# Hybrid decoder trunk on one core: RG gates by 64 rows, next convolutions between a pair's recurrences, joined masks and forget gate operand, an earlier weight split, another order at the end

## What is computed

```python
proj = h @ w_in         # RG x | RG gate | stick-breaking qkv | forgetting qkv | 8 forget logits | 3 merge gates
xa = causal_depthwise_conv4(rg_x) + b
r = sigmoid(block_diag(xa, w_a, b_a)); i = sigmoid(block_diag(xa, w_x, b_x))   # 16 blocks of 64 x 64
log_a = -8 * r * softplus(-lam); a = exp(log_a)
u = sqrt(-expm1(2 * log_a)) * (i * xa)
h_t = a_t * h_(t-1) + u_t                           # scan over the positions
ya = gelu(rg_gate) * h
yb = stick_breaking_attention(q, k, v)              # 8 heads of 64, strictly causal, no softmax
yc = forgetting_attention(q, k, v, log_sigmoid(fox_f + bf))   # softmax, plus the summed log forget gates
mixed = g0 * (ya @ w_rg) + g1 * (yb @ w_sb) + g2 * (yc @ w_fox)
```

## Time and profile before

| what | value |
|---|---|
| runs before | 2701.96 us median of 3 (2695.99 to 2702.55) |
| the profiled execution | 2708.77 us, its span 2707.0 us |
| mean granted TensorE clock | 0.997 |
| TensorE busy | 2655.9 us |
| VectorE, ScalarE, GpSimd busy | 1238.8, 1061.0, 1174.7 us |
| loads | 323.80 MB, mean 120 GB/s |

### The profile page before, as it was taken

How to read it: one execution, slowest core, us unless ns; L and a number is a source line. 1 busy time by engine, 2 the same in 40 slices (tenths; PEclk the granted TensorE clock), 3 DMA queues, 4 the chain that set the end, 5 groups by cost and what they waited for, 6 DMA issues and landing times.

```text
span 2707.0 us, 31703 instructions
## 1 busy us (share of the span) xinstructions
PE 2655.9 (98%) x13074; PEld 2236.0 (83%) x13074; DVE 1238.8 (46%) x1586; ACT 1061.0 (39%) x1596; POOL 1174.7 (43%) x476
## 2 busy tenths in 40 slices
PE   7999999999999999999999999999999999999998
PEld 5888897888888888888888888878888888888887
DVE  6555337866443244411155552578645422453111
ACT  6232245654443253222252222566543442522223
POOL 5555434523223435545345554444223234355442
PEclk9999999999999999999999999999999999999999
DMA  8555532222122224423245555222212122253332
GB/s 307 195 192 188 179 116 86 86 70 66 64 67 71 94 88 168 158 94 101 94 164 192 198 194 171 94 78 87 70 63 71 63 78 94 90 192 129 99 99 78
DMA packets 90832, 323.80 MB, mean 120 GB/s; under 512 B 10048, under 2 KB 12480, under 8 KB 90432
## 3 DMA queue, kind: packets, MB, share of 16 engines
q1 hardware_dynamic: 90688, 321.78, 35.2%
HBM read 319.64 MB, written 2.10 MB: 119 GB/s over the span
## 4 chain that ended last, share of the span: by engine, by line
PE 89%; DVE 6%; ACT 3%; DMA 1%; issue 1%; SPq 0%; POOL 0%; ACTq 0%; DVEq 0%
PE bank L1381 27%; PE bank L1383 27%; PE bank L1382 27%; PE bank L1419 2%; DVE e_lo L1203 2%; PE bank L1568 1%; DVE e_hi L1201 1%; PE bank L1424 1%; DVE e_f L1196 1%; DMA ada<-ada_w 1%; PE bank L1615 1%; PE bank L1580 1%; ACT h_hi L595 0%; ACT w_hi L540 0%; PE bank L1601 0%
## 5 line engine op out<-in xcount | busy, mean ns | idle before, releaser
L484 POOL TENSOR_TENSOR w_lo<-raw,w_hi 128x1024 fp32r<-128x1024 f32 x434 | 1129.6, 2614 | 1401.4 <-ACT w_hi L540 1401.0
L1381 PE MATMUL bank<-h_hi,w_hi 128*128 128x512 f32 x2224 | 868.7, 391 | 1.1 <-DVE tmp L1022 0.9
L1383 PE MATMUL bank<-h_hi,w_lo 128*128 128x512 f32 x2224 | 866.0, 389 | 0.0
L1382 PE MATMUL bank<-h_lo,w_hi 128*128 128x512 f32 x2224 | 866.0, 389 | 0.0
L540 ACT ACTIVATE w_hi<-raw 128x1024 fp32r<-128x1024 f32 x434 | 458.1, 1057 | 941.2 <-PE bank L1383 870.3
L1381 PEld LDWEIGHTS bank<-h_hi,w_hi 128*128 128x128 f32 x2224 | 418.1, 188 | 87.8 <-DVE tmp L1022 1.3
L1383 PEld LDWEIGHTS bank<-h_hi,w_lo 128*128 128x128 f32 x2224 | 417.8, 188 | 87.4
L1382 PEld LDWEIGHTS bank<-h_lo,w_hi 128*128 128x128 f32 x2224 | 418.1, 188 | 86.0
L944 DVE CUSTOM_DVE_ANT_0 ada<-ada,c_act 128x1024 f32<-128x1024 f32 x144 | 235.7, 1644 | 279.1 <-DMA ada<-ada_w 279.1
L1381 PE MATMUL bank<-g_hi,w_hi 128*128 128x512 f32 (+1 forms) x792 | 290.1, 366 | 0.0
L1383 PE MATMUL bank<-g_hi,w_lo 128*128 128x512 f32 (+1 forms) x792 | 289.4, 365 | 0.0
(11 more groups left out here) (243 smaller groups left out, 3119.6 us busy)
## 6 DMA issues: line engine op xcount, KB each, us to landing
raw<-w_units SPq DMA_DIRECT2D x440, 512.0 KB, 3.4
ada<-ada_w SPq DMA_DIRECT2D x144, 512.0 KB, 4.5
ada<-ada_w SPq DMA_DIRECT2D x8, 1024.0 KB, 17.1
x<-x_in SPq DMA_DIRECT2D x4, 512.0 KB, 6.4
wab_raw<-wab SPq DMA_DIRECT2D x2, 1024.0 KB, 5.6
y<-fin SPq DMA_DIRECT2D x8, 256.0 KB, 2.2
c_act<-c_rows SPq DMA_DIRECT2D x1, 512.0 KB, 3.7
vec<-vecs SPq DMA_DIRECT2D x3, 92.5 KB, 3.2
```

The source lines that it names most:

```text
L484: nc.gpsimd.tensor_tensor(w_lo[s][:, :, :], raw[u % RAW][:, :, :], w_hi[s][:, :, :].bitcast(F32), ALU.subtract).then_inc(unit_lo.sem, 1)
L1381: nc.tensor.matmul(o, wh, xh, start=start, stop=False, skip_group_check=True)
L1382: nc.tensor.matmul(o, wh, xl, start=False, stop=False, skip_group_check=True)
L1383: return nc.tensor.matmul(o, wl, xh, start=False, stop=stop, skip_group_check=True)
```

## The change

1. `gates`: the block-diagonal matrices become one [128, 128] operand per tile. Rows 0 to 63 hold block 0 of w_a and then of w_x, rows 64 to 127 block 1 of w_x and then of w_a. Six matmuls of 64 rows, alternating between the two row halves, write to two banks: r and i of block 0 in one, i and r of block 1 in the other. `gates_done` counts twice per tile. ScalarE takes r and i by four sigmoids of 64 partitions; the bias of i is rolled by 64 partitions on the host. The wab load, its `wab_hi` copy and `wab_lo` subtract are half as large.
2. VectorE's `rg_2`: recurrence of the pair's first tile, then the next pair's two convolutions (for the last pair `q_rest` and `k_rest`), then recurrence of the second tile. `forget_2` follows `rg_2(l, 0)`.
3. Forget gate: `wf_hi` and `wf_lo` become two column ranges (0 to 7 and 32 to 39) of one operand `wf` of 40 columns, zeroed once at the start. 16 matmuls instead of 24; VectorE adds the two row ranges of bank 7.
4. `scores`: the two diagonal blocks that lie in one bank get their mask by one matmul of 256 columns. For stick-breaking pairs three mask matmuls per head instead of four; for forgetting pairs the same, behind four with decay.
5. ScalarE: the tick of `U_WRG(2p)` moves from `q_round(l, p + 1)` to before `sb_1(l, p, 0)`.
6. End: `last_half`, `square` and `square_add` of the second half stand behind all eight tiles of the first half.

The diff, cut to its core:

```diff
@@ scalar: rg_2 @@
-                    act.wait_ge(gates_done.sem, gates_done.at(l, c + 1))
+                    act.wait_ge(gates_done.sem, gates_done.at(l, 2 * c + 2))
...
-                    A(gr[s][:, :], bank[b][:, :], ACT.Sigmoid, bias=vec[:, V_BA + c:V_BA + c + 1])\
-                        .then_inc(r_ready.sem, 1)
-                    A(gi[s][:, :], bank[b + 1][:, :], ACT.Sigmoid, bias=vec[:, V_BX + c:V_BX + c + 1])\
-                        .then_inc(i_ready.sem, 1)
+                    first, second = slice(0, HD), slice(HD, P)
+
+                    for src, bnk in ((first, b), (second, b + 1)):
+                        i = A(gr[s][src, :], bank[bnk][src, :], ACT.Sigmoid, bias=vec[src, V_BA + c:V_BA + c + 1])
+                    i.then_inc(r_ready.sem, 1)
+
+                    for dst, src, bnk in ((first, second, b), (second, first, b + 1)):
+                        i = A(gi[s][dst, :], bank[bnk][src, :], ACT.Sigmoid, bias=vec[src, V_BX + c:V_BX + c + 1])
+                    i.then_inc(i_ready.sem, 1)
@@ scalar: q_round, and the loop over the stick-breaking pairs @@
-                if 1 <= p <= 4:
-                    tick(l, u - 1)
...
                 for p in range(4):
+                    tick(l, U_WRG(2 * p))
                     sb_1(l, p, 0)
@@ scalar: end @@
-                    if h == 0 and k == 3:
-                        square(DEPTH - 1, 2, KD - 1, 1)
+                if h == 0:
+                    square(DEPTH - 1, 2, KD - 1, 1)
@@ vector: rg_2 @@
-                for c in both:
+
+                def recur(c):
...
-                    if c == KD - 2:
-                        q_rest(l, 0)
-                        k_rest(l, 0)
+
+                recur(c0)
+                if c0 + 2 < KD:
+                    rg_1(l, c0 + 2)
+                    rg_1(l, c0 + 3)
+                else:
+                    q_rest(l, 0)
+                    k_rest(l, 0)
+                recur(c0 + 1)
@@ vector: forget_1 @@
-                V.tensor_scalar(fx_a[:, :], bank[7][0:HEADS, :], b, None, ALU.add).then_inc(fx_step.sem, 1)
+                V.tensor_copy(fx_c[:, :], bank[7][QUAD:QUAD + HEADS, :]).then_inc(fx_low.sem, 1)
+                dve.wait_ge(fx_low.sem, fx_low.at(l, 1))
+                V.scalar_tensor_tensor(out=fx_a[:, :], in0=bank[7][0:HEADS, :], scalar=b, in1=fx_c[:, :], op0=ALU.add,
+                                       op1=ALU.add).then_inc(fx_step.sem, 1)
@@ vector: start, layer loop @@
+            V.memset(wf[:, :, :].bitcast(F32), 0.0).then_inc(wf_zero.sem, 1)
...
+                rg_1(l, 0)
+                rg_1(l, 1)
+                forget_1(l)
                 for c in range(0, KD, 2):
-                    rg_1(l, c)
-                    rg_1(l, c + 1)
+                    rg_2(l, c)
                     if c == 0:
-                        forget_1(l)
-                    if c == 2:
                         forget_2(l)
-                    rg_2(l, c)
@@ vector: end @@
-                    if h == 0 and k == 3:
-                        last_half(DEPTH - 1, 1)
-                    if h == 0 and k == 5:
-                        square_add(DEPTH - 1, 2, KD - 1, 1)
+                if h == 0:
+                    last_half(DEPTH - 1, 1)
+                    square_add(DEPTH - 1, 2, KD - 1, 1)
@@ tensor: gates @@
-                for j in range(2):
-                    i = mm3(bank[4 + 2 * (c % 2) + j][:, :], wab_hi[c % 2][:, j, :], wab_lo[c % 2][:, j, :],
-                            xa_hi[c % 2][:, :], xa_lo[c % 2][:, :], True, True)
-                i.then_inc(gates_done.sem, 1)
+                weights, x_a = (wab_hi[c % 2], wab_lo[c % 2]), (xa_hi[c % 2], xa_lo[c % 2])
+                for lp, rp in ((0, 0), (0, 1), (1, 0)):
+                    for j, r in enumerate((slice(0, HD), slice(HD, P))):
+                        i = nc.tensor.matmul(bank[4 + 2 * (c % 2) + j][:, :], weights[lp][r, :], x_a[rp][r, :],
+                                             start=lp == rp, stop=lp == 1, skip_group_check=True)
+                        if lp == 1:
+                            i.then_inc(gates_done.sem, 1)
@@ tensor: scores, for each head e @@
-                    for i in order:
...
+                    z = [bank[b] for b in ZB[e]]
+                    if p < 4:
+
+                        add(z[1].rearrange("p (i t) -> p i t", i=TT)[:, 0:4:3, :], ident_r[:, :],
+                            mask_sb[:, :].unsqueeze(1).to_broadcast([P, 2, P]))\
+                            .then_inc(z_done.sem, 1)
+                        for b in (2, 0):
+                            add(z[b][:, 0:P], ident_r[:, :], mask_sb[:, :]).then_inc(z_done.sem, 1)
+                    else:
+                        h = pick[:, 2 * p + e - HEADS:2 * p + e - HEADS + 1].to_broadcast([P, P])
+                        add(z[0], h, decay[:, :])
+                        add(z[0][:, 3 * P:], ident_r[:, :], mask_fx[:, :]).then_inc(z_done.sem, 1)
+                        add(z[1][:, 0:3 * P], h, decay[:, 0:3 * P])
+                        add(z[1][:, 3 * P:], h, decay[:, 0:P])
+                        add(z[1][:, 2 * P:], ident_r[:, :], mask_fx[:, :].unsqueeze(1).to_broadcast([P, 2, P])).then_inc(z_done.sem, 1)
+                        add(z[2][:, 0:2 * P], h, decay[:, 0:2 * P])
+                        add(z[2][:, P:2 * P], ident_r[:, :], mask_fx[:, :]).then_inc(z_done.sem, 1)
@@ tensor: forget gate @@
-                    i = mm3(bank[7][0:HEADS, :], wf_hi[:, k, :], wf_lo[:, k, :], h_hi[:, k, :], h_lo[:, k, :], k == 0,
-                            k == KD - 1)
+                    nc.tensor.matmul(bank[7][0:QUAD + HEADS, :], wf[:, k, :], h_hi[:, k, :], start=k == 0, stop=False,
+                                     skip_group_check=True)
+                    i = nc.tensor.matmul(bank[7][0:HEADS, :], wf_hi[:, k, :], h_lo[:, k, :], start=False,
+                                         stop=k == KD - 1, skip_group_check=True)
```

More of the change, by code:

```diff
@@ L150, in at, with trunk @@
         return count
-def trunk(nc, w_units, ada_w, vecs, wf, wab, c_rows, x_in, out):
+def trunk(nc, w_units, ada_w, vecs, wf_in, wab, c_rows, x_in, out):
     with ExitStack() as ctx:
@@ L230, in trunk @@
         gt = [at(f"gt{i}", 45056 + 2048 * i, [P, T]) for i in range(2)]
-        wab_raw = at("wab_raw", 65536, [P, KD, 2, P])
-        wab_hi = [at(f"wab_hi{i}", 73728 + 1024 * i, [P, 2, P], F32R) for i in range(2)]
-        wab_lo = [at(f"wab_lo{i}", 75776 + 1024 * i, [P, 2, P], F32R) for i in range(2)]
+        wab_raw = at("wab_raw", 65536, [P, KD, P])
+        wab_hi = [at(f"wab_hi{i}", 73728 + 1024 * i, [P, P], F32R) for i in range(2)]
+        wab_lo = [at(f"wab_lo{i}", 75776 + 1024 * i, [P, P], F32R) for i in range(2)]
         xa_hi = [at(f"xa_hi{i}", 77824 + 2048 * i, [P, T], F32R) for i in range(2)]
@@ L321, in trunk @@
         hl_0 = sig("hl_0")
+        wf_zero = sig("wf_zero")
         wfh = sig("wfh", 1)
@@ L441, in _ @@
                         sp.wait_ge(unit_done.sem, unit_done.at(l, U_RG))
-                        sp.dma_start(wab_raw[:, :, :, :], wab[l]).then_inc(wab_loaded.sem, 16)
+                        sp.dma_start(wab_raw[:, :, :], wab[l]).then_inc(wab_loaded.sem, 16)
                     if u == U_FFN[1] + 1:
@@ L1569, in scores, with add @@
                                              start=o == 0 and lp == 0 and rp == 0, stop=False, skip_group_check=True)
+                def add(dst, left, right):
+                    return nc.tensor.matmul(dst, left, right, start=False, stop=False, skip_group_check=True)
                 for e in range(2):
-                    for i in order:
-                        b, o = (SB_AT if p < 4 else FX_AT)[i]
-                        w = T - P * i if p < 4 else P * (i + 1)
-                        dst = bank[ZB[e][b]][:, o:o + w]
-                        if p < 4:
-                            last = nc.tensor.matmul(dst[:, 0:P], ident_r[:, :], mask_sb[:, :], start=False, stop=False,
-                                                    skip_group_check=True)
-                        else:
-                            h = 2 * p + e - HEADS
-                            nc.tensor.matmul(dst, pick[:, h:h + 1].to_broadcast([P, P]), decay[:, 0:w], start=False,
-                                             stop=False, skip_group_check=True)
-                            last = nc.tensor.matmul(dst[:, P * i:w], ident_r[:, :], mask_fx[:, :], start=False,
-                                                    stop=False, skip_group_check=True)
-                        if (b == 0) or (b == 2) or o == 384:
-                            last.then_inc(z_done.sem, 1)
@@ L1873, in _layout @@
     wf = np.stack([g["w_in"][l][:, f0:f0 + HEADS].reshape(KD, P, HEADS).transpose(1, 0, 2) for l in range(DEPTH)])
-    wab = np.zeros((DEPTH, P, KD, 2, P), np.float32)
+    wab = np.zeros((DEPTH, P, KD, P), np.float32)
     for j, name in enumerate(("rg_wa", "rg_wx")):
@@ L1878, in _layout @@
         for b in range(2):
```

(6 more changed lines are left out.)

32 lines of the change are left out of this document (17 added, 15 removed).

## The result

The changed kernel takes 2687.36 us (median of 4 runs, 2686.28 to 2689.24). The kernel before takes 2702.26 us beside it (median of 4 runs, 2695.99 to 2708.46). The ratio is 0.9946, 95% interval 0.9922 to 0.9969: faster by 0.54%, 14.9 us. Forecast were 2668 us, 34 us less than before, in a range of 2658 to 2683. The later runs were timed in three groups. The kernel before, timed beside each, had medians of 2703.12, 2702.05 and 2702.16 us, so medians of different groups can be set against each other to about 1 us. The profiled execution took 2686.28 us, its span is 2684.6, 22.4 us shorter than that of before (2707.0).

A forecast was written before the change was run, and what follows sets the result against it. TensorE, busy 98% of the span, was the bound. Terms 13.7 + 3.7 + 5.8 + 3.8 + 9.4 + 0.7 - 3.0 = 34.1 us took the profiled 2708.8 to 2674.7; less the 6.8 us offset, 2668 us, range 2658 to 2683.

The forecast's parts named there:

- Next convolutions between the recurrences: RG stage, VectorE: tile 2's xa_lo comes sooner, so TensorE's wait and slow clock go in both layers; 13.7 us won.
- Forget gate operand: Forget gate on TensorE: 16 matmuls instead of 24 save 1.85 us a layer, 3.7 us in all.
- Joined masks: Scores on TensorE: one mask matmul less per head, two per pair, 16 pairs; 3.8 us won, bounds 1.9 and 3.8.
- Sooner split: Stick-breaking pairs: moved split ends the wait for e_lo at suffix(1), 8 x 1.17 = 9.4 us won, bounds 0 and 9.4.
- Gates by 64 rows: RG gates on TensorE: a tile takes 1.00 us, not 1.36, with 0.30 for transitions; 5.8 us won over 16 tiles.
- New wait at the first w_rg: End of RG stage: TensorE waits for the last ya_lo, 1.5 us a layer (bounds 0 and 3.2); 3 us lost.
- End order: Kernel end: four fin operations no longer delay ScalarE's logarithm after the last square sum; 0.7 us won.
- (b): Split still collides: suffix(1) waits as before, w_rg wait reaches 3.2 us; 9.4 + 3.4 less won, 2681 us; chance 0.15.
- (a): Gates' row groups don't overlap or drain at every step: 10.6 us less won, 2678.5 us; chance 0.08.
- (c): Better than forecast: free transitions in the gates and no wait at w_rg, 4.7 + 3 more, 2660 us; chance 0.10.
- (d): Slower: VectorE becomes the bound of the RG stage, each of 8 pairs ends in a wait; 2737 us; chance 0.03.
- (e): Order changes do nothing, as another producer holds the same matmuls: 23 us of the sum go, 2691 us; chance 0.04.

The follow-up runs named there:

- The first undoing: Changed kernel with pair 0's split of the w_rg unit put back behind both heads' logarithms in each layer, pairs 1 to 3 kept early: 2679.11 us.
- the last two runs: Product tmp moved ahead of two ada tiles in layer 1's first network: on the changed kernel 2684.61 us; with pair 0's split also late 2676.94 us.

## Why the prediction was wrong

The direction was right. The gain was forecast at 34.1 us; it is 22.4 us between the two profiled executions, 14.9 us between the medians. The median is 19.4 us above the forecast. Two steps and one thing left out make most of it: the wait at the first w_rg (6.1 us more than priced), a wait in layer 1's network that isn't in the sum (3.5), and the step from the profiled execution to the median (7.6). Step by step:

- **Next convolutions between the recurrences: right.** 13.7 us forecast, 14.2 measured by the steps, 14.1 by undoing it between medians (15.7 between traces). No wait stands in its place in the RG stage. The slow stretches in the earlier trace rows were read 5.6 and 3.0 us long; they last 6.8 and 3.4, of which 5.7 and 3.4 lie behind the wait, so the slow clock cost 4.6 us and not 4.3.
- **Forget gate operand: right.** 3.7 forecast, 3.6 measured.
- **Joined masks: right.** 3.8 forecast, 0.238 a pair. Measured are 0.18 to 0.21 a pair, about 3.1 us, the forgetting pairs being as good as the others. The 0.119 of a mask was the mean of eight with the longer first one; the others start 0.111 us apart.
- **Sooner split: right** as to e_lo, 9.4 us by the steps. The wait at w_rg that it causes is counted below.
- **Gates by 64 rows: somewhat oversized.** 5.8 forecast, 4.0 measured. The transitions cost 0.40 us a tile, not 0.30: I had left out that the first 128-row matmul behind the pairs holds its place too long as well (420.99 to 421.32, 0.33 us instead of 0.227). The rule of the Trainium skill, "TensorEngine Tiling (Array Packing)" (Tiling Modes, Key Properties), that a change of the tiling mode drains the engine, agrees with these rows.
- **New wait at the first w_rg: of the terms of the sum this one failed most.** I took 1.5 us a layer from bounds of 0 and 3.2. The wait was 3.1 us, close to the upper bound. My reason for the lower one, that the split must first wait for its weights, was no protection: they landed 1.76 us after ScalarE was free, which put w_lo exactly beside the cast. The slack of 0.88 us in the earlier trace rows became a wait of 3.12 by 2.03 (cast), 1.65 (sigmoids, priced at 1.38) and about 0.3 (masks and gates, priced at 0.6), 4.0 in all. And I priced this wait without the slow clock that I had myself priced behind the xa_lo waits: 1.4 to 1.5 us more per layer. So 9.1 us were lost where I counted 3.0. The first undoing shows the part of the split, the 128-row gates that of the sigmoids.
- **Not in the prediction at all: 3.5 us in layer 1's first network**, 1.8 of wait and 1.7 of slow clock. The loads there are 1.75 us longer in flight, and the ada tiles hold up the product. Shown are the way from the landing to TensorE (the last two runs), and that the wait follows the time in flight through all traces. That the instruction load beside them makes them slow is what all eleven traces agree with; it was not undone by itself. The prediction had no term for what the change does to the place of loads, so this much is chance.
- **End order:** 0.7 us forecast, 0.6 measured.
- **The offset to the median: wrong.** The sum was taken over to the medians as if the profiled execution's 6.8 us above it were a constant of the kernel. Executions of the kernel before lay near 2696, 2702.5 or 2709 us, those of the changed one between 2686.3 and 2689.2. The profiled one was of the upper group, so part of the gain seen between the traces is not one of the median: 6.5 us above its median before, 1.1 us below after, so 22.5 - 7.6 = 14.9. The kernel with the old order of recurrences still spreads from 2695.6 to 2703.5, each kernel with the new order by at most 4.0 us. So the spread goes with the old order, and with it the xa_lo waits. The slow clock behind them explains only a part of it. Over the 35 executions timed beside the later runs the mean granted clock (each on record to 0.001) is 0.999 in the group near 2696, 0.9975 in that near 2702.5 and 0.9969 in that near 2709. If all of that difference fell on matmuls, it would be 4 and then 2 us (0.0015 and 0.0007 of 2700), where the groups are 6.4 and 6.5 apart. What the rest is stays open.

Measured terms: 14.2 + 3.6 + 4.0 + 2.7 + 9.4 + 0.6 - 9.1 - 3.5 = 21.9, and with the 0.4 at the start 22.3, against 22.4 in the spans. (2.7 are the masks of 14 pairs; those of the pairs 0 are inside the 9.1.) Of the rivals, (b) had the wait of 3.2 us at w_rg right, 3.4 us of its price, but the e_lo wait was gone, which was the other 9.4; (a), (c), (d) and (e) did not occur. The range of 2658 to 2683 would have held the gain of 22.4 us counted from the median (2679.9); the offset put the time outside.

## What to carry to other kernels

When an engine arrives sooner at a place, list every producer that it will meet there and add up what the change does to that producer's chain, a neighbour on the shared path included: 0.88 us of slack was used up by three additions that were each known. Price every new wait of TensorE with the slow clock that the same trace shows behind waits of its length, as a cost that may or may not come. And if single executions of a kernel lie in groups, find out in which the profiled one is before a gain in its trace is carried over to the median. Where a load lands late, look at its time in flight and at the other queues beside it before blaming the order of issue.

## What the runs showed of the hardware

- A VectorE cast of 128x512 took 0.43 us alone and 2.46 to 2.60 beside GpSimd's w_lo of 2.38 us; the scan took 1.23 and 3.27, the ada tile 1.22 and 3.38. The Trainium skill, "SBUF — State Buffer" (Who interferes with whom), states a rule for the cast: the port pair that VectorE and GpSimd share goes to whichever issues first, for its whole instruction. The rows agree: the cast starts 0.21 us after its w_lo (552.30) and ends at 554.97, w_lo ends at 554.68.
- Going over to 64-row matmuls and back cost 0.40 us beyond the pairs' own 0.70, 0.10 of it at the first 128-row matmul behind them.
- ScalarE's sigmoid of 64 partitions takes as long as that of 128, 0.69 us at 512 columns; a tile's four halves took 2.80 us from the first start to the operation behind them, two wholes 1.15. Of these 1.65 us a tile only the last tile's came onto the chain.
- After the first 40 us of a kernel and ahead of its end, the granted clock fell to 1.2 GHz at waits of TensorE of 6.1, 5.2, 4.7 (twice), 3.3, 3.2 (twice), 3.1 (three times), 2.9 (twice), 2.7, 2.3 (twice) and 2.2 us, and stayed at 2.4 GHz at others of 2.7, 2.8, 1.6, 1.3, 1.1 us and less. The fall came between 2.3 us before TensorE started again and 1.2 us after. The slow stretch was 3.4 us long, or 6.8 in four cases (waits of 6.1, 5.2, 4.7 and 3.2 us). At a wait of 2.7 us it went either way, in two kernels at the same place, and where it fell it cost 1.7 us more.
- A load of 512 KB for VectorE took 4.4 and 4.6 us from issue to landing where no instruction load of 16 KB lay beside it, and 5.1 to 6.3 us in the nine traces where one did.
